# Keys, values and conv rows leave by channel, decode's key products move into their own head, and the last phase reloads rows ahead of weights

## The reference, cut to what matters

```
h = rmsnorm(x)                                     # 2048 channels
q_a,k_a,v_a,z_a, qkv_b,z_b, beta,a = split(h @ w_in)
# mixer A, 8 heads x 128: rotary on q,k; windows (128,1),(512,4),(2048,16)
o_a = softmax attention over prompt tokens / over cache + own token
# mixer B, 8 heads x 128: causal conv (width 4) + SiLU, L2 norm, delta rule
c = silu(conv([conv_buf, qkv_b]));  S = decay*S + k (x) beta*(v - k.S);  o_b = rmsnorm(q.S)
y = x + rmsnorm(concat(o_a * silu(z_a), o_b * silu(z_b)) @ w_out)
```

## Time and profile before

| | |
|---|---|
| time, median of 3 runs | 1330.18 us (1328.22 to 1330.28) |
| the profiled execution | 1330.15 us |
| its span, first to last instruction | 1328.3 us |
| PE busy | 1258.6 us, 95% |
| DVE, ACT, POOL busy | 768.2, 543.2, 288.5 us |
| mean granted clock of TensorE | 0.984 |
| distance of one head to the next | 131.1 or 132.7 us |

### The profile page before, as it was taken

The page is one execution under the profiler, slowest core; times in us unless marked ns, Lnnn a source line. Parts: engine busy times, 40 slices in busy tenths (PEclk is TensorE's granted clock), DMA queues, the critical chain, the costliest instruction groups (busy, mean ns, idle before and its releaser), DMA issues. The chain is left out here.

```text
span 1328.3 us, 28169 instructions
## 1 busy us (share of the span) xinstructions
PE 1258.6 (95%) x10094; PEld 1212.4 (91%) x10094; DVE 768.2 (58%) x1872; ACT 543.2 (41%) x1472; POOL 288.5 (22%) x271
## 2 busy tenths in 40 slices
PE   4999998999999999999999999999999998899997
PEld 4989998999899989998999899989998997889997
DVE  6466367537653765377537653765376556474445
ACT  6352344434443444344434443444344444412210
POOL 1123112321232123212321232123112311122210
PEclk9999999999999999999999999999999998899998
DMA  6331434243324342434243324332434254312353
GB/s 226 92 96 51 137 105 146 55 146 108 129 55 147 106 130 58 138 113 136 66 138 111 122 66 138 116 118 66 138 117 132 66 185 143 98 65 95 95 192 129
DMA packets 82695, 151.71 MB, mean 114 GB/s; under 512 B 8793, under 2 KB 27330, under 8 KB 81026
## 3 DMA queue, kind: packets, MB, share of 16 engines
q1 hardware_dynamic: 72222, 144.87, 34.2%
q10 hardware_dynamic: 10384, 5.50, 1.6%
HBM read 132.20 MB, written 17.27 MB: 113 GB/s over the span
## 5 line engine op out<-in xcount | busy, mean ns | idle before, releaser
L553 PE MATMUL PJ<-h_hi,w_hi 128*128 128x264 f32 (+1 forms) x2432 | 723.3, 297 | 1.2 <-ACT memx L981 1.2
L554 PE MATMUL PJ<-h_lo,w_hi 128*128 128x264 f32 (+1 forms) x2432 | 689.9, 284 | 0.0
L555 PE MATMUL PJ<-h_hi,w_lo 128*128 128x264 f32 (+1 forms) x2432 | 688.3, 283 | 0.0
L553 PEld LDWEIGHTS PJ<-h_hi,w_hi 128*128 128x128 f32 x2432 | 462.5, 190 | 17.8 <-issue 12.4
L554 PEld LDWEIGHTS PJ<-h_lo,w_hi 128*128 128x128 f32 x2432 | 462.7, 190 | 2.8 <-issue 1.7
L555 PEld LDWEIGHTS PJ<-h_hi,w_lo 128*128 128x128 f32 x2432 | 460.9, 190 | 0.0
L1858 POOL TENSOR_TENSOR w_lo<-w_raw,w_hi 128x512 fp32r<-128x512 f32 x160 | 210.1, 1314 | 887.8 <-ACT w_hi L954 887.8
L954 ACT ACTIVATE w_hi<-w_raw 128x512 fp32r<-128x512 f32 x320 | 197.7, 624 | 102.7 <-PE PJ L555 84.1
L1364 DVE TENSOR_TENSOR w_lo<-w_raw,w_hi 128x512 fp32r<-128x512 f32 x160 | 114.0, 718 | 117.5 <-ACT w_hi L954 113.9
L981 ACT ACTIVATE memx<-PJ 128x264 f32<-128x264 f32 (+2 forms) x130 | 49.2, 379 | 71.9 <-PE PJ L555 60.5
L1223 ACT ACTIVATE mem<-MX 128x256 f32<-128x256 f32 x48 | 18.4, 384 | 116.6 <-PE MX L755 116.0
(11 more groups left out here) (317 smaller groups left out, 1618.8 us busy)
## 6 DMA issues: line engine op xcount, KB each, us to landing
w_raw<-in_w_in SPq DMA_DIRECT2D x256, 256.0 KB, 2.7
w_raw<-in_w_out SPq DMA_DIRECT2D x64, 256.0 KB, 2.8
kv<-in_cache_win_k SPq DMA_DIRECT2D x24, 512.0 KB, 3.6
kv<-in_cache_win_v SPq DMA_DIRECT2D x16, 512.0 KB, 3.8
mem<-in_x_prompt SPq DMA_DIRECT2D x4, 1024.0 KB, 10.4
S<-in_state_delta SPq DMA_DIRECT2D x8, 512.0 KB, 3.5
out<-S SPq DMA_DIRECT2D x8, 512.0 KB, 3.7
out<-mem ACTq DMA_DIRECT2D x16, 256.0 KB, 3.3
```

The costliest lines, as they stand in the source:

```text
L553: pe.matmul(out, wh, h_hi[:, k, tok], start=k == 0, stop=False)
L554: pe.matmul(out, wh, h_lo[:, k, tok], start=False, stop=False)
L555: last = pe.matmul(out, wl, h_hi[:, k, tok], start=False, stop=k == KT - 1)
```

## The change

Four things change. Line numbers with "after" are those of the changed file.

1. The outputs for keys, values and conv rows are now by channel. SP sends `xk` and `xv` (128 x 520) at eighths 53 and 58 and 11 columns of `xq` at eighths 9, 17 and 25, straight from where the projection put them; the host turns the arrays. The transposes of k, of q's and v's samples and of the conv rows, their copies and ten DMA issues of ACT's queue per head are gone. The samples' queries go to `scratch_q` by a DMA that transposes as it writes (eighth 46), in 1024 runs of 4 bytes. The four transposes of v remain for the attention, at eighth 60 instead of 59. ACT and DVE wait for the outputs to have left before they write over `xq`, `xa`, `xk`, `xv`.
2. Decode's key products (`decode_keys`, L1690 after) run at eighths 55, 56, 57, 58, 61 and 62 of their own head. SP loads `keys(0)` at eighth 47, `qb` at 49, `keys(1)` at 50, `keys(2)` at 57 and the values at 60 and at eighth 1 of the next head. The softmax stays at eighth 17 of the next head, but DVE's list has it last. The later sums move two eighths ahead.
3. Row 9 of the gated results moves into the buffer that the transposed keys no longer need, and so into the first group.
4. In the last phase SP lets the generators issue before its weight loads, and head 7's decode is 14 turns earlier on PE, ACT and DVE (`late=-14`).

```diff
-ROW_GROUPS = ((0, 1, 2, 3, 4, 5, 6, 8), (9, 10, 11), (12, 13, 14))
+ROW_GROUPS = ((0, 1, 2, 3, 4, 5, 6, 8, 9), (10, 11), (12, 13, 14))
...
@@ sync
             def attn_decode(hh):
-                yield from idle(8)
-                sp.wait_ge(s["red"], 3 * hh + 1)
-                sp.dma_start(K_TILE[2]..., cache_k[hh, 2]).then_inc(s["kb2_in"], 16)
...
+                yield
                 sp.wait_ge(s["red"], 3 * hh + 3)
...
             def attn_rows(h):
-                yield from idle(51)
...
+                yield from idle(47)
+                if not first:
+                    sp.wait_ge(s["pv_sum"], h)
+                keys(0)
                 yield from idle(2)
                 sp.wait_ge(s["qrow_out"], 16 * h + 16)
-                sp.dma_start(qb[:], scratch_q[h].partition_broadcast(P)).then_inc(s["qb_in"], 16)
+                sp.dma_start(qb[:], scratch_q[h].rearrange("b d -> (b d)").partition_broadcast(P)).then_inc(s["qb_in"], 16)
+                yield
+                if not first:
+                    sp.wait_ge(s["pv_ps"], h)
+                keys(1)
+                yield from idle(7)
+                sp.wait_ge(s["red"], 3 * h + 1)
+                keys(2)
...
+            def conv_out(h):
+                yield from idle(9)
+                for j in range(3):
+                    sp.wait_ge(s["proj_sb"], 16 * h + (2 * j + 4))
+                    sp.dma_start(c_new[h, j], xq[:, TP:3 + TT]).then_inc(s["crow_out"], 16)
+                    yield from idle(8)
+
+            def attn_out(h):
+                yield from idle(46)
+                sp.wait_ge(s["q_ok"], h + 1)
+                sp.dma_start(scratch_q[h].rearrange("b d -> d b"), xa[:, TP:TT],
+                             allow_slow_non_contiguous=True).then_inc(s["qrow_out"], 16)
+                yield from idle(7)
+                sp.wait_ge(s["k_ok"], h + 1)
+                sp.dma_start(k_new[h], xk).then_inc(s["k_out"], 16)
+                yield from idle(5)
+                sp.wait_ge(s["proj_sb"], 16 * h + 16)
+                sp.dma_start(v_new[h], xv).then_inc(s["v_out"], 16)
...
-                for k in (4, 5):
+                for k in (4, 5, 9):
                     load_row(k)
...
             for n in range(40):
+                step(work)
                 if n % 2 == 0 and n < 8 * PARTS:
                     wait_lo(T_O + slot + 1, p)
                     load_out(slot + 2, p)
-                step(work)
@@ tensor
             def own_a(h):
-                yield from idle(53)
...
-                for c in range(NC):
-                    pe.transpose(MD[:, 0, c * P:(c + 1) * P], xk[:, c * P:(c + 1) * P], ident[:])
-                pe.transpose(MD[0:NB, 1, 0:P], xa[:, TP:TT], ident[:])
-                pe.transpose(MD[0:NB, 1, P:2 * P], xk[:, TP:TT], ident[:]).then_inc(s["k_T"], 1)
-                yield from idle(6)
+                yield from idle(60)
                 pe.wait_ge(s["proj_sb"], 16 * h + 16)
...
                 for c in range(NC):
-                    pe.transpose(MD[:, 0, c * P:(c + 1) * P], xv[:, c * P:(c + 1) * P], ident[:])
-                pe.transpose(MD[0:NB, 1, 0:P], xv[:, TP:TT], ident[:]).then_inc(s["v_T"], 1)
+                    last = pe.transpose(MD[:, 0, c * P:(c + 1) * P], xv[:, c * P:(c + 1) * P], ident[:])
+                last.then_inc(s["v_T"], 1)
...
-            def own_b(h):
-                for j in range(3):
-                    yield from idle((11, 7, 8)[j])
...
-                    pe.transpose(MD[0:11, 1, 0:P], xq[:, 3 + TP - 3:3 + TT], ident[:]).then_inc(s["crow_ps"], 1)
...
-            work = [later(tail_a(NH - 1)), attn_decode(NH - 1)]
+            work = [later(tail_a(NH - 1)), attn_decode(NH - 1, late=-14)]
@@ vector
-            def attn_decode(hh, sums=(9, 1, 4)):
-                yield from idle(7)
-                dve.wait_ge(s["qb_in"], 16 * hh + 16)
+            def decode_keys(h):
+                yield from idle(55)
+                dve.wait_ge(s["qb_in"], 16 * h + 16)
                 for n in range(3):
-                    yield from idle((0, 3, 2)[n])
+                    yield from idle((0, 0, 2)[n])
...
-                stretch(h, [tail_a(h - 1), attn_decode(h - 1, sums=(24, 4, 3)), own_b(h), own_a(h), mix_b(h), mix_q(h),
-                            delta_decode(h)])
+                stretch(h, [tail_a(h - 1), mix_b(h), own_b(h), own_a(h), mix_q(h), delta_decode(h),
+                            attn_decode(h - 1, sums=(22, 4, 3)), decode_keys(h)])
```

More of the change, by code:

```diff
@@ L518, in _ @@
             sp.wait_ge(s["h_lo_ok"], H_READY + KT + 2)
+            sp.wait_ge(s["k_out"], 16 * NH)
             for c in range(NC):
@@ L845, in delta_decode, with attn_decode @@
                               stop=True).then_inc(s["d_outer"], 1)
-            def attn_decode(hh, sums=12):
-                yield from idle(17)
-                pe.wait_ge(s["vtok_ok"], 2 * hh + 2)
+            def attn_decode(hh, late=0, sums=12):
+                yield from idle(17 + late)
+                pe.wait_ge(s["vtok_ok"], hh + 1)
                 pe.wait_ge(s["qkp"], hh + 1)
@@ L870, in _ @@
             first_tiles()
-            stretch(0, [gates(), own_b(0), own_a(0), mix_b(0), mix_q(0), delta_decode(0)], first=1)
+            stretch(0, [gates(), own_a(0), mix_b(0), mix_q(0), delta_decode(0)], first=1)
             for h in range(1, NH):
-                stretch(h, [tail_a(h - 1), attn_decode(h - 1, sums=28), own_b(h), own_a(h), mix_b(h), mix_q(h),
+                stretch(h, [tail_a(h - 1), attn_decode(h - 1, sums=26), own_a(h), mix_b(h), mix_q(h),
                             delta_decode(h)])
@@ L1171, in own_b @@
             def own_b(h):
-                for j, m in enumerate((1, 2, 0)):
-                    yield from idle((11, 4, 5)[j])
-                    act.wait_ge(s["crow_ps"], 3 * h + j + 1)
-                    if j > 0 or not isinstance(h, int) or h > 0:
-                        act.wait_ge(s["crow_out"], 32 * (3 * h + j))
-                    act.activation(rows, MD[0:11, 1, 0:P], ACT.Copy).then_inc(s["crow_ok"], 1)
-                    yield
+                for j in range(3):
+                    yield from idle((12, 5, 6)[j])
                     act.wait_ge(s["conv_ok"], 3 * h + j + 1)
@@ L1261, in delta_decode, with attn_decode @@
                     s["d_rows_ok"], 1)
[L1263 to L1267 removed]
+            def attn_decode(hh, late=0, lag=0, gap=0):
+                yield from idle(18 + late)
                 act.wait_ge(s["sc_max"], hh + 1)
@@ L1723, in attn_decode @@
                     last.then_inc(s["red"], 1)
-                yield
-                yield
+                    yield
+            def attn_decode(hh, late=0, sums=(9, 1, 4)):
+                yield from idle(17 + late)
                 dve.wait_ge(s["sc_T"], hh + 1)
@@ L1979 @@
     r = run_bass_kernel_spmd(nc, [arrays], core_ids=[0])
-    return tuple(r.results[0][f"out_{i}"] for i in range(len(_OUTS)))
+    return tuple(np.ascontiguousarray(a) for a in outputs(*(r.results[0][f"out_{i}"] for i in range(len(_OUTS)))))
```

120 lines of the change are left out of this document (40 added, 80 removed).

## The result

The changed kernel takes 1385.31 us (median of 4 runs, 1382.98 to 1387.58) against 1330.23 us of the kernel before: a ratio of 1.0415, with an interval of 1.0393 to 1.0437. It is 55 us slower, where 27 us faster were forecast. The profiled execution took 1385.66 us with a span of 1383.8 us; TensorE's mean granted clock is 0.964, against 0.984.

What follows compares the result with a forecast made beforehand. PE, busy 95% of the span, was taken to bound the kernel; terms of -7.0 + 3.5 - 5.8 - 4.2 - 5.4 - 7.9 = -26.8 us gave 1303.4 us from 1330.18, with a range of 1296 to 1314.

Steps and rivals of the forecast that it cites:

- By these rows it lands in 2.0 to 3.7 us; I take 3.: Scatter of q's samples, issued at eighth 46: lands in 3 us, before SP wants it at eighth 49, so free.
- the scatter is slow: Rival, chance 0.05: scatter delays qb's load at eighth 49; past 9 us, each further us costs 8 us over the heads.
- Transposes that leave, -7.0: PE, each head: eight removed transposes at 0.11 us save 0.88 us, -7.0 us over eight heads.
- v's behind L802, +3.5: PE, eighth 60: v's four transposes, hidden before, are paid openly, 0.44 us a head; L802's wait grows to 0.70.
- First decode wait, -5.8: PE at L854: its 0.8 us wait for scores in seven heads goes, since products run in the head before.
- holds no removed operation: DVE's chain behind L727's 2.42 us wait is untouched, so that wait stays and swallows the third conv row's saving.
- Second decode wait, -4.2: PE at L858: most of its 0.62 us wait, 4.4 us in seven heads, goes; 0 is the other bound.
- The margin of 0.2 us: At L858: DVE is through at 603.7 at the latest, PE comes at 603.9; the margin was called small.
- Products at 0: Key products at eighths 55 to 62 fit DVE's idle time and cost nothing; bound 27 us if PE paid in full.
- Last phase, first part, -5.4: Start of last phase: late rows issued earlier cut 16.4 us to 11.0, including 1.3 to 2 us waiting for h_lo.
- Last phase, second part, -7.9: Head 7's decode sums at L865: moved between units, -6.4 us; the next unit no longer at half clock, -1.5 us.
- The clock: PE's falls to half clock, 1.5 us each, in five of seven distances, kept; rival that all go: 1296, chance 0.10.

Runs made afterwards that it cites:

- e8: e1 plus an idle transfer at eighth 46 of 1024 runs of 64 bytes, which nothing reads: 1326.63 us.
- e12: e1 plus an idle scatter at eighth 46 of 1024 runs of 4 bytes, each landing 64 bytes from the next: 1325.13 us.
- e1: Changed kernel, but the samples' queries go to DRAM in 128 runs of 32 bytes and DVE reads qb with a stride: 1327.94 us, ratio to before 0.998.
- e6: e1 with v's four transposes at eighth 59, ahead of mixer B's last ones: 1323.87 us.
- e10: e7 with the key products and their loads back in the next head (products at eighths 7 to 15): 1350.09 us.
- e5: e1 with mixer B's part behind the convolutions and attention's own part (rotary) in DVE's list: 1326.04 us.
- e9: e6 with mixer B's part behind the convolutions but ahead of attention's own part in DVE's list: 1306.09 us, ratio to before 0.9816.
- e14: e9 with decode's softmax ahead of the convolution again in DVE's list: 1306.17 us.
- e7: e1 with head 7's decode in the last phase 14 turns later again on PE, ACT and DVE: 1333.24 us.
- e13: e1 plus an idle scatter at eighth 46 of 128 runs of 4 bytes (one sample), side by side: 1383.65 us.

## Why the prediction was wrong, step by step

**The step that failed: "By these rows it lands in 2.0 to 3.7 us; I take 3."** It took 12 us, and its landing was the smaller part. I bounded the scatter by transfers with as many or longer runs, and e8 and e12 show that such transfers are harmless indeed. What sets this one apart, neighbouring words from different partitions, is in no row of the kernel before. My rival "the scatter is slow" had the sign and 0.05; but it put the harm at `qb`'s load, where 12 us of landing would have cost 24 us and left the kernel near 1327. The harm is at every transfer under way in the next 12 us, of either queue, whoever waits for it. The one that hurts is the swap in ACT's queue, with DVE's and PE's chain behind it: DVE waits 7.5 us for it and PE 5.1, in each head. The cost is 57 us (e1). The sum had the scatter down as free. The two rules that I had weighed don't tell it apart either. The Trainium skill, DMA: Bandwidth & Descriptors, says in "Specifications" that a transfer below 512 bytes is read, modified and written, and in "Rules for kernel authors" that a non-contiguous last dimension becomes one descriptor for each element. Both hold for e12's 1024 single elements as well, and these cost nothing.

**Transposes that leave, -7.0, and v's behind L802, +3.5.** Right: L806 waits 0.70 us as worked out, and e6 gives 4.1 us for the second.

**First decode wait, -5.8.** The wait is gone. The 1.0 us more at L727's place is not its heir (e10) but comes from the order of DVE's list (e5, e9). I had read from the trace that the chain "holds no removed operation", but not that with mixer B's masks put ahead, the convolution's end meets POOL's split (617.38 in e1, 3.9 us after DVE's own split; before, 618.32, which is 6.9 us after it). +7.6 us in eight heads, and longer stretches at half clock.

**Second decode wait, -4.2.** Wrong: 5.9 us in place of 4.4. The margin of 0.2 us (603.7 against 603.9) was taken from the upper end of my own 2 to 2.8 us; from the lower end DVE is through at 604.5, behind PE. I had allowed one meeting with POOL, in the convolution's piece; it comes instead at the softmax's small instruction that makes `dg`, which takes 1.15 us in place of 0.22 (at 606.08 us of e1), right ahead of what PE waits for. e14 shows the place of the softmax as the cause (the wait goes with it), and the time stays the same.

**Products at 0.** Right in the heads: no wait of PE behind them in e1. At the joint to the last phase they cost 3.4 us, as the next term shows. (The words of my bound are off: 5.1 us less the 1.7 us of the two groups inside the idle of 4.75 is 3.4.)

**Last phase, first part, -5.4.** Right by itself, but spoilt by the products. From the last L805 of head 7 to the end, e1 takes 1326.7 - 1093.55 = 233.2 us where before took 1328.3 - 1087.62 = 240.7: 7.5 us less, against 13.3 (12.9 after v's transposes). e7 and e10 tell where the rest went, since both have head 7's decode as late as before. Their value sums start at

```profile
1161.41 3.57 PE L868 MATMUL MD<-ones,kv 128*128 128x1 f32 x16 [4.65 <-DVE kv L1719]
```

```profile
1174.83 3.58 PE L868 MATMUL MD<-ones,kv 128*128 128x1 f32 x16 [4.65 <-DVE kv L1719]
```

which is 65.6 us after the last L805 in e7 (1095.81) and 62.2 us in e10 (1112.64). Before, it was 68.2 (1155.84 - 1087.62). So the early rows bring 6.0 us in e10, where the products stand in the last phase as before, and only 2.6 in e7, where they stand in head 7. The rows are there, but the first unit waits for `h_lo` behind the last eight products; DVE, then PE in e1:

```profile
1098.17 1.52 DVE L1689 CUSTOM_DVE_ANT_0 kv<-kv,qb 128x128 f32<-128x128 f32 x1
1099.62 0.40 DVE L1689 CUSTOM_DVE_ANT_0 kv<-kv,qb 128x128 f32<-128x128 f32 x1
...
1102.67 0.35 PE L890 MATMUL PJ<-h_hi,w_hi 128*128 128x256 f32 x1 [2.21 <-DVE h_lo L1740]
```

In e10 PE has no wait for `h_lo` in the last phase. I had a wait of 1.3 to 2 us in the sum, but not that it falls on the first unit, so that in e1 the next 4 us run at half clock. (In the changed kernel it is 1.35 us, and the clock stays at 1.00 behind it.)

**Last phase, second part, -7.9.** The mechanism is right and the size somewhat high: 5.3 us between the medians of e1 and e7. The profiles give 6.9 (240.1 against 233.2 us behind the last L805), but e7's profiled execution was the slowest of its ten.

**The clock.** I had kept its falls as they were. In e1's profile it falls in every head and for longer, behind a wait at L730 that grew from 2.4 to 3.4 us; in e9's it hardly falls. The length of the wait does not settle it alone, as e8 and e12 show. Between e1 and e9 lie 21.9 us, of which the waits themselves (L730 and L805, 6.7 and 3.3 us) are less than half.

So a time near the sum could be had, 1306.1 us in e9 against 1303.4, but not by the terms of the sum. e9 lacks the second decode wait's 4.2 us and half of the last phase's 13.3. It gains instead from v's transposes back at eighth 59 and from a clock that hardly falls, which the forecast had as a rival at 0.10. That the two numbers lie close is in part luck.

## What to carry to other kernels

A transfer is priced by what it does to others: look at every wait for DMA of any queue in the 10 us around it. A scatter that writes neighbouring 4 byte words as separate runs from different partitions is to be avoided, even with 128 words; let each partition write its own run (32 bytes were enough here) and give the stride to the engine that reads. If instructions change order on an engine, its partners' next instructions move as well; so check what they now collide with, and count a lengthened wait together with the matmuls at half clock behind it.

## What the hardware showed that I had not expected

- 128 words of 4 bytes, written side by side from 128 partitions, land after 9.7 us, and 1024 after about 12; other transfers nearly stand meanwhile (the swap of 32.5 KB takes 10.2 us in the head of e13 shown above, in place of 2.0). 64 bytes apart, 1024 words land in 3.7 us.
- A strided read (32 bytes from one element to the next) slows DVE's product of 128x128 from 0.28 to 0.40 us (before and e1).
- With a wait of 0.84 us taken away ahead of a wait of 2.5 us, the clock fell behind the second one in six of seven heads instead of two (e14 against e9, one profile each). In e8 and e12 it falls in some heads and not in others behind the same wait. So a short wait that is removed need not be won, and one profile does not settle what a fall costs a kernel.
